# Where five pieces of the expert ring and the expert stage's small buffers lie in SBUF, and when the first loads may start

## The reference

```python
h = concat(meta_tokens, x)
h = h + rms_norm(rglru_block(rms_norm(h)))            # layer 0: gated linear recurrence
h = h + rms_norm(swiglu(rms_norm(h)))                 # dense channel mixer, 3072 wide
k_nope, k_rope, v = shared_latent_kv(h)
h = h + rms_norm(mla_block(rms_norm(h), k_nope, k_rope, v))   # layer 1: attention, 16 heads
# mixture of experts: softmax over 8 experts, top 2, gate weights renormalised
y = 0
for ex in range(8):
    y = y + gate[:, ex:ex + 1] * swiglu(u, w_gate_up[ex], w_down[ex])   # (1024 x 7168), (3584 x 1024)
h = h + rms_norm(y)
return h[:, 16:]
```

## Time and profile before

| | us |
|---|---|
| runs | 1359.32, 1353.38, 1359.0 (median 1359.0) |
| the profiled execution's own time | 1354.27 |
| its span, first to last instruction | 1351.8 |
| TensorE busy | 1292.5 (96%) |
| VectorE, ScalarE, GpSimd busy | 421.0, 348.3, 54.5 |
| mean DMA rate over the span | 313 GB/s |
| TensorE clock over the span | 0.991 of full |

### The profile page before, as it was taken

The page is one execution under the profiler, slowest core; times in us unless marked ns, Lnnn a source line. Parts: engine busy times, 40 slices in busy tenths (PEclk is TensorE's granted clock), DMA queues, the critical chain, the costliest instruction groups (busy, mean ns, idle before and its releaser), DMA issues.

```text
span 1351.8 us, 26196 instructions
## 1 busy us (share of the span) xinstructions
PE 1292.5 (96%) x11384; PEld 744.8 (55%) x11384; DVE 421.0 (31%) x804; ACT 348.3 (26%) x659; POOL 54.5 (4%) x81
## 2 busy tenths in 40 slices
PE   8989999999889899999999999999999989999986
PEld 7988999999788773443333443333443332343331
DVE  7785866653687641001010001000001000000102
ACT  7885544443567740000000000000000000000001
POOL 3001100001120020000000000000000000000000
PEclk9989999999989989999999999999999999999999
DMA  9538455555223289999999999999999999999994
GB/s 290 166 97 262 126 186 180 164 186 158 71 90 116 96 342 362 363 372 387 417 417 417 416 417 418 415 418 417 416 417 419 416 417 418 416 417 417 417 418 182
DMA packets 127954, 423.79 MB, mean 313 GB/s; under 512 B 8272, under 2 KB 77136, under 8 KB 99168
## 3 DMA queue, kind: packets, MB, share of 16 engines
q1 hardware_dynamic: 127664, 421.58, 80.4%
q0 software_dynamic: 176, 0.53, 0.1%
HBM read 421.03 MB, written 1.05 MB: 312 GB/s over the span
## 4 chain that ended last, share of the span: by engine, by line
PE 77%; DMA 8%; SPq 6%; DVE 5%; ACT 3%; issue 1%; DVEq 0%; ACTq 0%
PE bank L894 31%; PE bank L871 13%; PE bank L502 9%; PE bank L504 9%; PE bank L503 8%; SPq L1019 6%; DMA ring<-in_m_w_gate_up 4%; DMA ring<-in_m_w_down 3%; PE bank L849 1%; PE bank L830 1%; PE bank L861 1%; PE bank L863 1%; PE bank L694 1%; DVE w_lo L1519 1%; DVE rstd L1539 1%
## 5 line engine op out<-in xcount | busy, mean ns | idle before, releaser
L894 PE MATMUL bank<-ring,x_T 128*32 128x512 f32 (+1 forms) x5120 | 488.8, 540 | 9.6 <-DMA ring<-in_m_w_gate_up 8.2
L894 PEld LDWEIGHTS bank<-ring,x_T 128*32 128x32 f32 x5120 | 164.6, 110 | 328.7 <-issue 303.8
L871 PE MATMUL bank<-ring,eT 128*32 128x512 f32 x2240 | 247.3, 593 | 12.4 <-DMA ring<-in_m_w_down 12.4
L502 PE MATMUL bank<-u_hi,w_hi 128*128 128x272 f32 (+2 forms) x632 | 184.4, 292 | 7.0 <-DVE u_lo L1574 5.1
L504 PE MATMUL bank<-u_hi,w_lo 128*128 128x272 f32 (+2 forms) x632 | 182.2, 288 | 0.0
L503 PE MATMUL bank<-u_lo,w_hi 128*128 128x272 f32 (+2 forms) x632 | 181.6, 287 | 0.0
L1519 DVE TENSOR_TENSOR w_lo<-raw,w_hi 128x2048 fp32r<-128x2048 f32 (+7 forms) x89 | 143.9, 1638 | 95.3 <-ACT w_hi L1138 95.2
L871 PEld LDWEIGHTS bank<-ring,eT 128*32 128x32 f32 x2240 | 69.9, 110 | 181.2 <-issue 155.9
L2001 DVE TENSOR_TENSOR e_h<-bank,e_h 128x512 f32<-128x512 f32 (+1 forms) x40 | 22.7, 618 | 417.1 <-PE bank L894 417.1
L1138 ACT CAST w_hi<-raw 128x2048 fp32r<-128x2048 f32 (+7 forms) x89 | 117.9, 1352 | 52.9 <-PE bank L504 52.9
L502 PEld LDWEIGHTS bank<-u_hi,w_hi 128*128 128x128 f32 (+1 forms) x632 | 118.7, 188 | 11.3 <-issue 5.0
(11 more groups left out here) (302 smaller groups left out, 1168.8 us busy)
## 6 DMA issues: line engine op xcount, KB each, us to landing
ring<-in_m_w_gate_up SPq DMA_DIRECT2D x128, 1024.0 KB, 23.4
ring<-in_m_w_down SPq DMA_DIRECT2D x112, 1024.0 KB, 24.3
ring<-in_m_w_gate_up SPq DMA_DIRECT2D x128, 768.0 KB, 22.0
raw<-in_f_w_gate_up SPq DMA_DIRECT2D x24, 1024.0 KB, 5.3
raw<-in_f_w_down SPq DMA_DIRECT2D x12, 1024.0 KB, 5.3
raw<-in_a_w_in SPq DMA_DIRECT2D x10, 1024.0 KB, 8.5
raw<-in_a_w_out SPq DMA_DIRECT2D x8, 640.0 KB, 4.6
raw<-in_b_w_o SPq DMA_DIRECT2D x4, 1024.0 KB, 5.2
```

The lines of the kernel that those rows point to most:

```text
L502: nc.tensor.matmul(o, a[0], b[0], start=start, stop=False)
L871: return nc.tensor.matmul(strip(q, t, NT), eT[u][:, bank, P * i + GROUP * at:P * i + GROUP * at + GROUP], w[:, n, :], start=start, stop=stop)
L894: last = nc.tensor.matmul(strip(q + 3 * (kind_of == "up"), t, width), x_T[:, part, group(g)], w[:, width * n:width * n + width], start=(pa ...
```

## The change

The ring keeps its 17 x 2048 words but is laid in two tensors. `ring_low` holds 12 x 2048 words over `raw`, `w_hi` and `w_lo`. `ring_high` holds the five "own" pieces; it lies farther back, behind all the small buffers, over attention's keys, values and queries. The order of places in the ring is now: six pieces over `raw`, five in `ring_high`, six over `w_hi` and `w_lo`; no piece may straddle one of these borders. The expert stage's small buffers move to where the residual and its neighbours lay. For the first expert, pieces 6 to 10 now wait for the last head to be weighed, and pieces 11 to 16 for `b_out` 1, 2 and 3; no piece waits for `"logits"`.

```diff
-RING = 17 * CHUNK
+RING, RING_RAW, RING_OWN = 17 * CHUNK, 6 * CHUNK, 5 * CHUNK
+RING_ENDS = (RING_RAW, RING_RAW + RING_OWN, RING)
...
     for n in WORDS + WORDS:
-        if at % RING + n > RING:
-            at += RING - at % RING
+        end = min(e for e in RING_ENDS if e > at % RING)
+        if at % RING + n > end:
+            at += end - at % RING
...
-        ring = sb("ring", [P, RING])
+        ring_low = sb("ring_low", [P, RING - RING_OWN])
+        x_T = sb("x_T", [P, KD, CAP])
+        y_big = sb("y_big", [P, D])
+        y_part = sb("y_part", [P, NT])
+        selT_big = sb("selT0", [P, NB, P])
+        sel = sb("sel", [P, NB, CAP])
+        eT_0 = sb("eT0", [P, NGS[BIG], SECTIONS[0][1]])
+        e_h = sb("e_h", [P, NGS[BIG], NT])
+        grow = sb("grow", [P, D])
...
+        acc = sb("acc", [P, NB, D])
...
         h_tok = sb("h_tok", [P, NB, D])
         u_tok = sb("u_tok", [P, NB, D])
...
+        ring_high = sb("ring_high", [P, RING_OWN])
+        def ring_piece(kind, c):
+
+            at, n = OFFSETS[EC * kind + c], WORDS[c]
+            if at >= RING_ENDS[1]:
+                at -= RING_OWN
+            elif at >= RING_RAW:
+                return ring_high[:, at - RING_RAW:at - RING_RAW + n]
+            return ring_low[:, at:at + n]
...
                 elif c < RAW:
                     sp.wait_ge(lo_done, NC0 - RAW + c + 1)
-                elif c < RAW + 2 * SPLIT:
-                    at(sp, "chunk", NC0 - SPLIT + (c - RAW) // 2)
+                elif c < RAW + RING_OWN // CHUNK:
+                    at(sp, "weighed", HEADS - 1)
                 else:
-                    at(sp, "logits")
+                    at(sp, "chunk", min(NC0 - SPLIT + (c - RAW - RING_OWN // CHUNK) // 2, NC0 - 1))
```

More of the change, by code:

```diff
@@ L342, in yoco_kernel @@
         SC = [(0, META, META + P), (META + P + 16, 0, KX)]
-        ring = sb("ring", [P, RING])
+        ring_low = sb("ring_low", [P, RING - RING_OWN])
[7 more added lines that the diff above has]
+        grow = sb("grow", [P, D])
+        gated_sel = sb("gated_sel", [P, NB, CAP])
+        eT = [eT_0, sb("eT1", [P, NGS[BIG], SECTIONS[1][1]])]
+        acc = sb("acc", [P, NB, D])
+        y_small = sb("y_small", [P, D])
+        selT = [selT_big, sb("selT1", [P, NB, P])]
         h_tok = sb("h_tok", [P, NB, D])
         u_tok = sb("u_tok", [P, NB, D])
[L348 to L359, removed]
         queue = sb("queue", [P, 3, NB, NE])
         queue_next = sb("queue_next", [P, 3, NB, NE])
-        grow = sb("grow", [P, D])
         rbias = sb("rbias", [P, NE])
@@ L369, in yoco_kernel @@
         ordered = sb("ordered", [P, NE, NE])
+        ring_high = sb("ring_high", [P, RING_OWN])
+        final = ring_low[:, 0:NB * D].rearrange("p (b n) -> p b n", b=NB)
+        final_sq = ring_low[:, NB * D:2 * NB * D].rearrange("p (b n) -> p b n", b=NB)
+        def ring_piece(kind, c):
[5 more added lines that the diff above has]
+            return ring_low[:, at:at + n]
         landed = [sem(f"landed{i}") for i in range(RAW)]
@@ L808, in landed_chunk @@
                     pe.wait_ge(ring_landed[c % LANDINGS], ex * 32 + 16 * (c // LANDINGS + 1))
-                    at = OFFSETS[EC * kind + c]
-                    return ring[:, at:at + WORDS[c]]
+                    return ring_piece(kind, c)
                 def strip(q, t, width):
@@ L1009, in expert_loads @@
                     n0, width = SECTIONS[u]
-                    at = OFFSETS[EC * kind + c]
+                    dst = ring_piece(kind, c)
                     if kind_of != "down":
@@ L1013, in expert_loads @@
                         src = up[:, part, col:col + 4 * width]
-                        dst = ring[:, at:at + WORDS[c]]
                     else:
                         (n, i), (n2, i2) = part
-                        dst = ring[:, at:at + WORDS[c]].rearrange("p (r c) -> p r c", r=2)
+                        dst = dst.rearrange("p (r c) -> p r c", r=2)
                         src = tiles[u][:, n, i:i + 2, :] if n == n2 else tiles[u][:, n:n + 2, i, :]
```

## The result

The changed kernel takes 1359.3 us (median of 20 runs, 1357.3 to 1361.9), the kernel before 1356.35 us (20 runs, 1353.4 to 1359.3). The ratio is 1.0022, 95% interval 1.0015 to 1.0028: slower by 3.0 us. The profiled execution took 1359.8 us with a span of 1357.9.

A forecast was written before the change was run, and what follows sets the result against it. DMA bound the expert stage at 417 GB/s after its last hole, the end following from the loop's start. Terms 0 + 0 + 0 + 1.5 on 1356.6 gave 1358 us, range 1351 to 1365.

The forecast's parts named there:

- what sets the end: Expert stage: DMA saturates after its last hole, so the loop's start at 507.30 us, set by the router, fixes the end.
- the short landing: Expert stage: the last ring load landing after about 4 us comes 131 us after the loop's first matmul starts.
- five pieces earlier: First expert's pieces 12 to 16 load before the logits: 0 us at the end, at most 12.6 us gain.
- the order of the ring: Ring places with the new borders: one wait 1.9 us earlier, but 0 us in all, bounds -0.5 to +0.5 us.
- the small buffers: Moved buffers in expert stage and router: only addresses differ, 0 us, bounds -0.5 to +0.5 us.
- The DMA hole ahead of the first freed piece: Before the expert loop: early loads in by 503.2 us, then DMA idle from about 504 to 510 us.
- Who meets the loads now: +1.5 us: Router: grow and rbias share DMA engines with ring loads; rbias lands at 498.0 us, delaying VectorE's sum; bounds 0 to 7.9 us.
- the base: Whole kernel: starting time 1356.6 us, the middle of four known executions of the kernel before.
- The slower one: Router: grow and rbias wait out the ring's whole backlog, landing at 504.5 us; +7.9 us, 1364.5 us; chance 0.06.
- Its second half: Router: TensorE's clock falls in the longer pause and the gather's 3.78 us doubles, 1368 us; no separate chance.
- The faster rival: First expert's early loads: bytes moved ahead count, DMA saturated from 496.51 us on; 12.6 us gain, 1344 us; chance 0.04.
- rule of turns between queues: Router: DMA engines alternate queues by packet, so the small loads slip some 1 to 3 us, never 7.9 us.

The follow-up runs named there:

- the second profile: The changed kernel run and profiled again with no edit: 1359.3 us against 1356.1 for the kernel before, ratio 1.0026.
- uncoupled_same: Changed kernel, every address kept: rbias in unused columns of a small buffer, loaded early, grow awaited only at the end; 1355.7 us against 1356.5, ratio 0.9992.
- layout_only: Changed kernel's layout and ring borders, but the first expert's loads wait as in the kernel before; 1355.96 us against 1356.06, ratio 0.9995.
- bias_first: Changed kernel with rbias loaded ahead of grow on its own semaphore, grow awaited only at the end; 1355.1 us against 1356.5, ratio 0.9985.
- before_late: Kernel before with three more 512 KB copies of grow ahead on GpSimd's queue, VectorE waiting for all; 1360.45 us against 1356.5, ratio 1.0025.
- before_pad: Kernel before with an unused 32-byte buffer ahead of the weight buffers, ring at byte 24832; 1343.4 us against 1356.5, ratio 0.9901.
- uncoupled: Changed kernel with rbias in its own 32-byte buffer, loaded at the start, grow awaited only at the end; 1344.0 us against 1356.1, ratio 0.9911.
- after_pad: Changed kernel with an unused 32-byte buffer ahead of the weight buffers, ring's low part at 24832; 1346.3 us against 1356.5, ratio 0.9929.

## Why the prediction was right and wrong

**Right: what sets the end.** "The end is thus set by the moment TensorE reaches piece 4 of the first SMALL expert", and so by the loop's start. The column "rest" shows it, and the short landing came 131 us after the start, as foretold. The times themselves came later than the signs named, since the start did: the loop at 514.2 us and not 508 to 509, the last load in at 1342.9 and not 1338 us (511.0 and 1339.7 us in the second profile). One count in that part was off by a piece: before the load that follows the last hole, 62.5 pieces' worth had been issued and not 61.75, which is 1.9 us at the DMA rate and changes nothing in the forecast.

**Right: five pieces earlier, 0 us; the order of the ring, 0; the small buffers, 0.** `uncoupled_same` has all three and stands at 0.9992; `layout_only` has the last two and stands at 0.9995. The traces are finer: the new layout's rest is 0.6 to 0.8 us shorter, all of it between the issue of the last short load and the last landing (697.4 against 698.2 us), where DMA ran at 417.4 against 417.0 GB/s. That is just outside the bounds of 0.5 us put on these terms, and the reason given there, that no row shows an address to matter, did not last (see the last section). The DMA hole ahead of the first freed piece grew, as said: it lasted from 505 until the loop began. The seventeen pieces were in at 506.7 us, not 503.2; the sum had left out `grow`'s 1.3 us of transfer and the slow first two us (61 GB/s from 472 to 474 us).

**Right in kind, wrong in size: "Who meets the loads now: +1.5 us".** This is the step that failed, and it is a mis-sized term. I let `rbias` come "one ring piece later", at 498.0 us. It landed at 490.67 + 9.4 = 500.1 us, 4.6 us later than before and not 2.5. The mistake was to count turns only for `rbias`. It waits behind `grow` on its own queue, and `grow` itself, 512 KB, now took 8.7 us instead of 4.6, since all of it went through beside the ring's traffic. `rbias` landed 1.5 us behind it (498.6 and 500.1 us), hardly more than the 1.3 us of before (494.2 and 495.5 us). `bias_first` shows the converse: in front of `grow` it lands after 6.7 us, in time.

The sum's slip by traces: from the reciprocal of the root to the sum it took 10.35 us in the kernel before (486.26 to 496.61) and 13.6 (486.59 to 500.18) and 13.9 us in the two profiles of the changed kernel, so 3.2 to 3.5 us. In `layout_only`, where the sum doesn't wait for `rbias` either, it took 10.7 us, in `before_late` 15.2. Less the 0.8 us that the new layout gives back, the slip makes 2 to 3 us; the timed 3.0 us agree as well as these profiles allow. So the slip is the whole of the difference in the medians as far as can be told, and they leave no room for the further 3.3 us that the gather took in the first profile. The gather took 3.78 us only in the profile of the kernel before and 5.4 to 7.1 us in all others, late small loads or none. I had read one profile's 3.78 us as the kernel's own time. Had I compared the two first profiles alone, I should have told of a loss of 6 us where there are 3.

**Right: the base.** I started from the middle of four executions, 1356.6; twenty runs give 1356.35. The predicted 1358 lies 1.3 us under the measured 1359.3, nearly all of it the term above. The forecast called it "same", within 0.5%; it is a loss of 0.22% that twenty runs resolve, with the sign of the sum and twice its size. A measurement of twenty runs tells 0.07% here, not the half percent that the forecast reckoned with.

**The rivals.** The slower one, the whole backlog, would have put `rbias` at 504.5; it landed at 500.1, between the two. Its second half, the clock falling in the longer pause, did happen in the first profile and could not be told from what the clock does there anyway: in `layout_only` and `uncoupled_same`, without the longer pause, it was at half for part of the gather too. The faster rival is excluded by `uncoupled_same`.

From the Trainium skill's rule of turns between queues ("DMA: Bandwidth & Descriptors", Queues, rings and completion order) the prediction estimated a slip of 1 to 3 us and not 7.9, without showing how the 1 to 3 come out of it. The trace, with 3.2 to 3.5, is just above the upper end and far from the backlog's.

## What to carry to other kernels

In this kernel, loads moved ahead of a stage could pay only if the stage would have waited for them, or if the DMA engines never went idle afterwards. To tell which holds elsewhere: find the last short landing, and see what ends the hole before it. Before filling an idle stretch of the DMA engines, list every other load that is under way in it, with its deadline and what stands ahead of it on its own queue; a small load with 1 us of slack belongs ahead of a large one, on its own semaphore, or at the start of the program. And compare kernels with equal addresses: a small buffer put ahead of a large one can move the time more than the edit under study.

## What the hardware showed unasked

The DMA rate went with the start address of the ring, or of its low part: byte 24800 of a partition, 417 GB/s; 24768, 418; 24704, 419; 24832, 424 to 425 GB/s. The first three are 224, 192 and 128 past a multiple of 256, the last is one. In time that is 0, -2.5, -4 and -13 us. The trace holds every row of a load as a packet of its own. From 720 to 1300 us the mean packet of 8, 6 and 4 KB took 315.7, 239.4 and 162.2 ns in the kernel before, and 309.8, 234.6 and 159.2 ns in `before_pad`: 1.9, 2.0 and 1.9% less.

The Trainium skill ("DMA: Bandwidth & Descriptors", How a descriptor splits into AXI transactions) says, of what a descriptor reads, that each transaction starts at a multiple of 256 bytes, and that a descriptor which starts elsewhere begins with a transaction that is only partly used. Carried over to what is written, an estimate from that page is 33 transactions instead of 32 for a row of 8 KB and 17 instead of 16 for one of 4 KB: at most 3 and 6% more. The measured loss has that sign, and it falls with the bytes past the multiple. But it is no larger a share of a short row than of a long one, which the estimate does not foretell.

Nor does a row's own start settle it. In `uncoupled` the high part of the ring, 5 of 17 places, starts 64 past a multiple of 256, in `after_pad` 96 past one, and yet 94 and 97% of the 8 KB packets took the short 309 ns, though more than a quarter of them go to the high part. In `uncoupled_same`, with the high part at the very same address but the low part at 24800, the median of the 8 KB packets is 313 ns. With the high part off the multiple the rest is only 0.7 to 1.1 us longer (831.7 and 832.0 against 830.9 and 831.0), of 13 us in all. So the cause stays open; and the pad moved all buffers behind it, not the ring alone. Which buffer's start matters was not tried.
